# Summing the adaptive layer's weights on VectorE, 512 columns and one k-tile at a time, in place of GpSimd

## The chip, the cores and the metric

The kernel runs on one core of a Trainium2 chip, in one launch. The metric is device time in microseconds; the value of a kernel is the median of its runs. All times of single instructions below come from one execution that the hardware profiler took. The core's engines have one instruction queue each and wait for each other by semaphores: TensorE (PE) for matmuls, VectorE (DVE), ScalarE (ACT), GpSimd (POOL) and SyncE (SP, which here only issues DMAs).

## The reference

Two transformer blocks on 256 tokens of width 1024, all in float32. The first has two layers, each a feed-forward part, a mixer and another feed-forward part; the second is one layer of the same make, but every sublayer of it is modulated by a vector that comes from `c`. What the change touches is how that vector is made:

```python
mod = (jax.nn.silu(c) @ w_ada[l] + b_ada[l]).reshape(b, N_SUB, 3, D_MODEL)   # c: (1, 1024), w_ada[l]: (1024, 9216)
def sublayer(h, i, fn, resid_w):
    shift, scale, gate = mod[:, i, 0, None, :], mod[:, i, 1, None, :], mod[:, i, 2, None, :]
    u = rms_norm(h, norm_pre[l, i]) * (1.0 + scale) + shift
    return h + resid_w * gate * rms_norm(fn(u), norm_post[l, i])
h = sublayer(h, 0, ffn1, 0.5); h = sublayer(h, 1, token_mixer, 1.0); h = sublayer(h, 2, ffn2, 0.5)
```

The weights `w_ada` are 9216 columns of 1024 rows, 37.7 MB, used for one row of input.

## The kernel before

**Stages.** The program is a row of stages: six feed-forward stages of 11 chunks of 256 hidden columns, and the projections of the three mixers. A feed-forward stage is named here by the number of the norm ahead of it: norm 0, 2, 3, 5, 6 and 8. Norm 0, 2, 3 and 5 belong to the first block, norm 6 and 8 to the second.

**A chunk.** Each chunk takes three slots of weights of 128x2048 elements: slots 0 and 1 hold the up and gate weights, slot 2 the down weights. SP loads a slot into `raw`; ACT rounds it to `w_hi` (L1351, `split_hi`); DVE takes the rest, `w_lo` = `raw` - `w_hi` (L1875, `split_lo`); PE multiplies with three matmuls per product (L598 to L600, `three`). In one chunk PE runs `up` on slot 0 (24 matmuls), `up` on slot 1 (24) and `down` of the chunk before on slot 2 (24). DVE also multiplies the activated gate with the up half (L2038, `product`), transposes it by blocks (L2023, `blocks`), and, after four DMAs from ACT's queue and ACT's rounding (L1477), takes the rest of the turned hidden values, `hT_lo` (L2028, `turned_lo`). `middle(c)` writes DVE's order in one chunk: `w_lo` of slot 2, `hT_lo`, `w_lo` of slot 0, the two products, the transpose, `w_lo` of slot 1.

**The adaptive layer.** GpSimd works through 72 units of 128 columns. A unit is one DMA (L561, all eight k-tiles of the 128 columns, 512 KB) and four passes: multiply all 1024 elements of a partition by `c_silu` (L567), and add halves until 128 are left (L570, L572, L576). The loads alternate between two buffers, and unit n+2 is loaded when unit n is summed. Three units make 384 columns of `ada_acc`. DVE then folds them, in `fold(j)`: it waits for GpSimd's sum (`ada_summed`), transposes by blocks of 32 (L2047), and adds (L2050). There are 24 folds, six in each of the stages norm 2, 3, 5 and 6, after chunks 2, 3, 5, 6 and 8 (`FOLD_AT`) and after the last product. PE adds up what is left with four small matmuls (`ada_select`), at the start of the stages norm 5 and 6 and of the token mixer; the folds of a third must be done by then.

**When GpSimd works.** The first half of the units begins when the first mixer's output is turned for its projection and has 18 units before it waits for the stage norm 3 to begin (`actT_ready`), then 18 more; the second half does the same at the second mixer's output and at the stage norm 6.

**Queues.** Each engine takes its instructions in the written order. So a DVE fold that waits holds up every `w_lo` behind it, and `w_lo` is what PE waits for.

Of the kernel before, what the change touches and what calls it, by code (L numbers as in the profile page):

```python
# [167 lines left out]
def build(nc, a, out):  # L168
# [4 lines left out]
    with ctx:  # L173
# [173 lines left out]
        ada_scaled, ada_by4, ada_by2, ada_summed = (sem(n) for n in ("ada_scaled", "ada_by4", "ada_by2", "ada_summed"))  # L347
# [178 lines left out]
        def _(pool):  # L526
# [35 lines left out]

            def ada_unit(n):
                j, r = n // ADA_PER, ada_raw[:, n % 2, :, :]
                at = (n % ADA_PER) * ADA_U
                pool.wait_ge(ada_loaded[n % 2], 16 * (n // 2 + 1))
                nc.gpsimd.tensor_tensor(r, r, c_silu[:, :].unsqueeze(2).to_broadcast([P, KD, ADA_U]), ALU.mult)\  # L567
                    .then_inc(ada_scaled, 1)
                pool.wait_ge(ada_scaled, n + 1)
# [2070 lines left out]
```

## Time and profile before

| what | value |
|---|---|
| median of 3 runs | 1611.08 us (1610.66 to 1611.93) |
| span of the profiled execution, first to last instruction | 1609.3 us |
| what lies outside of the span, by the median of the runs | 1.8 us |
| PE busy | 98% |
| DVE busy | 72% |
| ACT busy | 51% |
| GpSimd busy | 38% |

The profiled execution's own time is not listed apart from the runs'; its span is 1.8 us under their median, and that distance is taken as what lies around a span. Busy shares are means over all stages. PE's instructions overlap in the records (each matmul is listed with about 390 ns and a new one begins every 226 ns or so), so PE counts as busy when it streams without a gap.

### The profile page before, as it was taken

What the parts mean: (1) busy time and instruction counts of PE and PEld (TensorE: products, weight loads), DVE (VectorE), ACT (ScalarE), POOL (GpSimd) and SP (SyncE); (2) the same over time, 40 slices, a digit from 0 to 9 for tenths busy, and PEclk for the clock granted to TensorE, in tenths of its full rate; (3) what the DMA queues carried; (4) which work ended last, traced back from release to release, by engine and by line L of the source; (5) the groups of instructions that cost most, each with busy time, mean ns of one, the idle gap of its engine ahead of it and who ended that gap; (6) DMA issues with size and microseconds to landing.
All of it is one profiled execution on the core that took longest, in us unless ns stands there. A gap on an engine that the chain in (4) does not pass through costs nothing.

```text
span 1609.3 us, 20974 instructions
## 1 busy us (share of the span) xinstructions
PE 1580.6 (98%) x7549; PEld 1303.2 (81%) x7549; DVE 1157.7 (72%) x1123; ACT 821.7 (51%) x984; POOL 615.5 (38%) x387
## 2 busy tenths in 40 slices
PE   7999999999999999999999999999999999999998
PEld 6888888888888788887887888888887888878887
DVE  5665668778877787876778787688798467775554
ACT  6465563354444544455665444554437566564443
POOL 2000100077993599930009898079992000000000
PEclk9999999999999999999999999999999999999999
DMA  8766663358887688865346889668884454447662
GB/s 268 232 208 214 215 209 105 105 174 274 268 276 222 207 277 262 271 198 191 124 139 220 282 257 282 217 192 272 259 278 162 156 174 146 170 144 222 205 219 86
DMA packets 242396, 337.25 MB, mean 210 GB/s; under 512 B 14185, under 2 KB 180290, under 8 KB 242336
## 3 DMA queue, kind: packets, MB, share of 16 engines
q1 hardware_dynamic: 196288, 281.05, 53.2%
q0 software_dynamic: 11280, 39.56, 7.9%
q10 hardware_dynamic: 34768, 15.83, 4.0%
q8 instruction: 37, 0.61, 0.2%
q14 instruction: 23, 0.19, 0.0%
HBM read 319.62 MB, written 1.05 MB: 199 GB/s over the span
## 4 chain that ended last, share of the span: by engine, by line
PE 79%; DVE 8%; POOL 6%; ACT 3%; issue 2%; DMA 1%; ACTq 1%; SPq 0%; DVEq 0%; POOLq 0%
PE ps L598 23%; PE ps L600 23%; PE ps L599 23%; DVE w_lo L1875 4%; PE ps L649 3%; POOL arena L570 2%; POOL arena L567 2%; PE ps L657 1%; PE ps L898 1%; ACT w_hi L1351 1%; PE ps L606 1%; POOL arena L572 1%; POOL arena L576 1%; DMA arena<-arena 1%; DVE arena L1907 1%
## 5 line engine op out<-in xcount | busy, mean ns | idle before, releaser
L1875 DVE TENSOR_TENSOR w_lo<-raw,w_hi 128x2048 fp32r<-128x2048 f32 x265 | 682.1, 2584 | 210.3 <-ACT w_hi L1351 209.8
L1351 ACT CAST w_hi<-raw 128x2048 fp32r<-128x2048 f32 x265 | 503.9, 1912 | 308.1 <-PE ps L600 255.7
L598 PE MATMUL ps<-w_hi,actT_hi 128*128 128x512 f32 x1456 | 572.0, 393 | 3.5 <-DVE w_lo L1875 2.5
L600 PE MATMUL ps<-w_hi,actT_lo 128*128 128x512 f32 x1456 | 567.0, 389 | 0.0
L599 PE MATMUL ps<-w_lo,actT_hi 128*128 128x512 f32 x1456 | 566.8, 389 | 0.0
L598 PEld LDWEIGHTS ps<-w_hi,actT_hi 128*128 128x128 f32 x1456 | 273.4, 188 | 63.4 <-issue 3.3
L600 PEld LDWEIGHTS ps<-w_hi,actT_lo 128*128 128x128 f32 x1456 | 273.3, 188 | 57.4
L599 PEld LDWEIGHTS ps<-w_lo,actT_hi 128*128 128x128 f32 x1456 | 273.5, 188 | 55.3
L570 POOL TENSOR_TENSOR arena<-arena 128x512 f32<-128x512 f32 x72 | 190.3, 2643 | 5.7
L567 POOL TENSOR_TENSOR arena<-arena,c_silu 128x1024 f32<-128x1024 f32 x72 | 153.6, 2133 | 100.6 <-DVE actT_lo L1910 49.9
L598 PE MATMUL ps<-w_hi,hT_hi 128*128 128x512 f32 x480 | 187.9, 391 | 1.6 <-DVE hT_lo L2028 1.6
L599 PE MATMUL ps<-w_lo,hT_hi 128*128 128x512 f32 x480 | 186.9, 389 | 0.0
L600 PE MATMUL ps<-w_hi,hT_lo 128*128 128x512 f32 x480 | 186.9, 389 | 0.0
L561 POOL DMA_DIRECT2D arena<-w_ada_dram x72 | 66.0, 917 | 295.7 <-PE ps L606 272.6
L2038 DVE TENSOR_TENSOR hidden<-gate,ps 128x256 f32<-128x256 f32 x132 | 76.7, 596 | 60.4 <-ACT gate L1486 53.9
L572 POOL TENSOR_TENSOR arena<-arena 128x256 f32<-128x256 f32 x72 | 109.5, 1521 | 5.6
L598 PEld LDWEIGHTS ps<-w_hi,hT_hi 128*128 128x128 f32 x480 | 90.1, 188 | 21.9 <-DVE hT_lo L2028 3.4
L600 PEld LDWEIGHTS ps<-w_hi,hT_lo 128*128 128x128 f32 x480 | 90.1, 188 | 18.9
L599 PEld LDWEIGHTS ps<-w_lo,hT_hi 128*128 128x128 f32 x480 | 90.1, 188 | 18.5
L1486 ACT ACTIVATE gate<-ps 128x256 f32<-128x256 f32 x66 | 25.3, 384 | 137.1 <-PE ps L600 116.7
L576 POOL TENSOR_TENSOR arena<-arena 128x128 f32<-128x128 f32 x72 | 80.4, 1117 | 17.4 <-DVE ada_fold L2050 12.0
L2028 DVE TENSOR_TENSOR hT_lo<-arena,hT_hi 128x512 fp32r<-128x512 f32 x60 | 72.8, 1213 | 4.2 <-ACT hT_hi L1477 4.1
(278 smaller groups left out, 1287.4 us busy)
## 6 DMA issues: line engine op xcount, KB each, us to landing
raw<-ffn_w_in_dram SPq DMA_DIRECT2D x174, 512.0 KB, 5.0
raw<-ffn_w_out_dram SPq DMA_DIRECT2D x88, 512.0 KB, 4.6
arena<-w_ada_dram POOLq DMA_DIRECT2D x72, 512.0 KB, 6.4
raw<-ffn_w_gate_dram SPq DMA_DIRECT2D x44, 512.0 KB, 4.0
raw<-ffn_w_up_dram SPq DMA_DIRECT2D x44, 512.0 KB, 5.1
raw<-ffn_w_down_dram SPq DMA_DIRECT2D x44, 512.0 KB, 4.4
raw<-w_in_dram SPq DMA_DIRECT2D x40, 512.0 KB, 4.8
raw<-hg_w_in_dram SPq DMA_DIRECT2D x32, 512.0 KB, 5.0
```

What stands on the lines that cost most here:

```text
L561: nc.gpsimd.dma_start(ada_raw[:, n % 2, :, :], w_ada[:, :, n * ADA_U:(n + 1) * ADA_U]).then_inc(ada_loaded[n % 2], 16)
L567: nc.gpsimd.tensor_tensor(r, r, c_silu[:, :].unsqueeze(2).to_broadcast([P, KD, ADA_U]), ALU.mult)\
L570: nc.gpsimd.tensor_tensor(r[:, 0:4, :], r[:, 0:4, :], r[:, 4:8, :], ALU.add).then_inc(ada_by4, 1)
L572: nc.gpsimd.tensor_tensor(r[:, 0:2, :], r[:, 0:2, :], r[:, 2:4, :], ALU.add).then_inc(ada_by2, 1)
L576: nc.gpsimd.tensor_tensor(ada_acc[j % 2][:, at:at + ADA_U], r[:, 0, :], r[:, 1, :], ALU.add).then_inc(ada_summed, 1)
L598: nc.tensor.matmul(to, hi, whi, start=start, stop=False, skip_group_check=True)
L599: nc.tensor.matmul(to, hi, wlo, start=False, stop=False, skip_group_check=True)
L600: return nc.tensor.matmul(to, lo, whi, start=False, stop=stop, skip_group_check=True)
L1351: nc.scalar.copy(w_hi[:, s, :], raw[:, s, :]).then_inc(hi_ready[s], 1)
L1875: nc.vector.tensor_tensor(w_lo[:, s, :], raw[:, s, :], w_hi[:, s, :].bitcast(F32), ALU.subtract)\
L2028: nc.vector.tensor_tensor(hT_lo.rearrange("p f t -> p (f t)").rearrange("p (n a j) -> p n a j", n=4, a=4), hT_columns, hT_hi.bitcast(F32). ...
L2038: nc.vector.tensor_tensor(to, g, u, ALU.mult).then_inc(hidden_ready, 1)
```

## The change

The unit is cut the other way. A unit is now two k-tiles of 512 columns (again 512 KB, again 72 units), and four units give 512 finished columns. For each k-tile DVE runs one pass over 512 columns: for the first of eight `ada_acc = part * c_silu[k]`, for the other seven `ada_acc = part * c_silu[k] + ada_acc`. That is 144 passes, 36 in each of the stages norm 2, 3, 5 and 6: one unit (two passes) in `middle(c)` between `hT_lo` and `w_lo` of slot 0, and one after `middle(c)`, for the chunks 1 to 9. Each pass waits for the one before it by `ada_added`, and the first of a unit for its load. A fold takes 512 columns; there are 18 of them, each right after the unit that ends its 512 columns, and none after the last product. GpSimd keeps only the 72 DMA issues, each after the unit two before it is added.

```diff
-ADA_U = 128
-ADA_PER = 3
-ADA_FOLD = ADA_PER * ADA_U
-FOLD_AT = (2, 3, 5, 6, 8)
+ADA_FOLD = 512
+ADA_KS = 2
+ADA_PER = KD // ADA_KS
+FOLDS = 3 * ADA_W // ADA_FOLD
+ADA_UNITS = FOLDS * ADA_PER
+ADA_IN = {2: 0, 3: 18, 5: 36, 6: 54}
...
-                pool.wait_ge(ada_loaded[n % 2], 16 * (n // 2 + 1))
-                nc.gpsimd.tensor_tensor(r, r, c_silu[:, :].unsqueeze(2).to_broadcast([P, KD, ADA_U]), ALU.mult)\
-                nc.gpsimd.tensor_tensor(r[:, 0:4, :], r[:, 0:4, :], r[:, 4:8, :], ALU.add).then_inc(ada_by4, 1)
-                nc.gpsimd.tensor_tensor(r[:, 0:2, :], r[:, 0:2, :], r[:, 2:4, :], ALU.add).then_inc(ada_by2, 1)
-                nc.gpsimd.tensor_tensor(ada_acc[j % 2][:, at:at + ADA_U], r[:, 0, :], r[:, 1, :], ALU.add).then_inc(ada_summed, 1)
...
+            for n in range(ADA_UNITS):
+                if n == ADA_UNITS // 2:
                     pool.wait_ge(turned, 4 * (by_name["fox_out"].turned + 1))
+                elif n % (ADA_UNITS // 2) >= 2:
+                    pool.wait_ge(ada_added, ADA_KS * (n - 1))
+                j, ks = n // ADA_PER, n % ADA_PER * ADA_KS
+                nc.gpsimd.dma_start(ada_raw[:, n % 2, :, :], w_ada[:, ks:ks + ADA_KS, j * ADA_FOLD:(j + 1) * ADA_FOLD])\
+                    .then_inc(ada_loaded[n % 2], 16)
...
+                def ada_add(n):
+                    acc_j = ada_acc[n // ADA_PER % 2]
+                    dve.wait_ge(ada_loaded[n % 2], 16 * (n // 2 + 1))
+                    for kk in range(ADA_KS):
+                        k, part = n % ADA_PER * ADA_KS + kk, ada_raw[:, n % 2, kk, :]
+                        if k == 0:
+                            total = nc.vector.tensor_scalar(acc_j, part, c_silu[:, k:k + 1], None, ALU.mult)
+                        else:
+                            dve.wait_ge(ada_added, ADA_KS * n + kk)
+                            total = nc.vector.scalar_tensor_tensor(acc_j, part, c_silu[:, k:k + 1], acc_j, ALU.mult, ALU.add)
+                        total.then_inc(ada_added, 1)
...
-                        middle(c)
+                        unit = ADA_IN[st.norm] + 2 * (c - 1)
+                        middle(c, lambda: ada_add(unit))
+                        ada_add(unit + 1)
...
-                        if c in FOLD_AT:
-                            fold(FOLD_IN[st.norm] + FOLD_AT.index(c))
+                        if unit % ADA_PER:
+                            fold(unit // ADA_PER)
```

VectorE's queue in chunk 2 of the stage norm 2, from `hT_lo` to the first fold and the `w_lo` of slot 2 behind it, before (`hi_ready0`, `1` and `2` name the slots; `arena<-arena` of 128x384 is the fold's transpose):

```order
L2028 TENSOR_TENSOR hT_lo<-arena,hT_hi 128x512 [waits hT_hi_ready]
L1875 TENSOR_TENSOR w_lo<-raw,w_hi 128x2048 [waits hi_ready0]
L2038 TENSOR_TENSOR hidden<-gate,ps 128x8x32 [waits gate_ready] x2
L2023 STREAM_TRANSPOSE arena<-hidden 128x512 [waits hT_loaded,hidden_ready]
L1875 TENSOR_TENSOR w_lo<-raw,w_hi 128x2048 [waits hi_ready1]
L2047 STREAM_TRANSPOSE arena<-arena 128x384 [waits ada_summed]
L2050 TENSOR_REDUCE ada_fold<-arena 128x12 [waits ada_block]
L1875 TENSOR_TENSOR w_lo<-raw,w_hi 128x2048 [waits hi_ready2,ada_folded]
```

Here nothing of the adaptive layer but the fold stands in the queue. And now, the same piece of the same chunk:

```order
L2003 TENSOR_TENSOR hT_lo<-arena,hT_hi 128x512 [waits hT_hi_ready]
L2031 SCALAR_TENSOR_TENSOR arena<-arena,c_silu 128x512 [waits ada_added,ada_loaded0]
L2031 SCALAR_TENSOR_TENSOR arena<-arena,c_silu 128x512 [waits ada_added]
L1850 TENSOR_TENSOR w_lo<-raw,w_hi 128x2048 [waits hi_ready0]
L2013 TENSOR_TENSOR hidden<-gate,ps 128x8x32 [waits gate_ready] x2
L1998 STREAM_TRANSPOSE arena<-hidden 128x512 [waits hT_loaded,hidden_ready]
L1850 TENSOR_TENSOR w_lo<-raw,w_hi 128x2048 [waits hi_ready1]
L2031 SCALAR_TENSOR_TENSOR arena<-arena,c_silu 128x512 [waits ada_added,ada_loaded1]
L2031 SCALAR_TENSOR_TENSOR arena<-arena,c_silu 128x512 [waits ada_added]
L2037 STREAM_TRANSPOSE arena<-arena 128x512 [waits ada_added]
L2040 TENSOR_REDUCE ada_fold<-arena 128x16 [waits ada_block]
L1850 TENSOR_TENSOR w_lo<-raw,w_hi 128x2048 [waits hi_ready2,ada_folded]
```

Two passes now stand ahead of slot 0's `w_lo` and two behind slot 1's, and the fold waits for VectorE's own passes and no longer for GpSimd's.

GpSimd's queue at the first unit, before, two loads ahead and then passes and loads in turn:

```order
L561 DMA arena<-w_ada_dram 128x8x128 [waits c_ready,turned]
L561 DMA arena<-w_ada_dram 128x8x128
L567 TENSOR_TENSOR arena<-arena,c_silu 128x1024 [waits ada_loaded0]
L570 TENSOR_TENSOR arena<-arena 128x512 [waits ada_scaled]
L572 TENSOR_TENSOR arena<-arena 128x256 [waits ada_by4]
L576 TENSOR_TENSOR arena<-arena 128x128 [waits ada_by2]
L561 DMA arena<-w_ada_dram 128x8x128 [waits ada_summed]
```

And now, both halves and the bias that follows them:

```order
L564 DMA arena<-w_ada_dram 128x2x512 [waits turned]
L564 DMA arena<-w_ada_dram 128x2x512
L564 DMA arena<-w_ada_dram 128x2x512 [waits ada_added] x34
L564 DMA arena<-w_ada_dram 128x2x512 [waits turned]
L564 DMA arena<-w_ada_dram 128x2x512
L564 DMA arena<-w_ada_dram 128x2x512 [waits ada_added] x34
L566 DMA arena<-da_bias_dram 128x1536
```

All four passes are gone from this queue, and what a load waits for is VectorE.

## Rows read from the trace of the kernel before

**Rows 1.** The page: span, then engines with busy us, share and instructions.

```profile
span 1609.3 us, 20974 instructions
PE 1580.6 (98%) x7549; PEld 1303.2 (81%) x7549; DVE 1157.7 (72%) x1123; ACT 821.7 (51%) x984; POOL 615.5 (38%) x387
```

**Rows 2.** Windows, inside norm 6 and norm 8: busy us (instructions) by engine, PEclk, DMA.

```profile
1053.00:1217.00 164.00, 161.29 (x716) 132.32 (x715) 134.72 (x87) 73.20 (x65) 153.13 (x89) 1.00 0.82 260
1440.00:1590.00 150.00, 150.00 (x663) 124.17 (x663) 88.94 (x66) 65.37 (x58) 0.00 (x0) 1.00 0.65 205
```

**Rows 3.** Waits of PE from 326 to 1222 us: total us, times, longest.

```profile
PE ps L606 <- DVE arena L1916: 2.0, 5, 0.4
PE ps L598 <- DVE w_lo L1875: 1.7, 1, 1.7
PE ps L598 <- DVE hT_lo L2028: 1.6, 3, 0.7
PE ps L706 <- DVE hidden L2038: 1.4, 1, 1.4
```

**Rows 4.** Timeline of VectorE at those waits: start, us, instruction [idle before].

```profile
348.21 1.77 DVE L1916 TENSOR_SCALAR arena<-x,small 128x1024 f32<-128x1024 f32 x1
...
364.29 3.43 DVE L1875 TENSOR_TENSOR w_lo<-raw,w_hi 128x2048 fp32r<-128x2048 f32 x1 [1.85 <-ACT w_hi L1351]
...
543.40 8.10 DVE L1875 TENSOR_TENSOR w_lo<-raw,w_hi 128x2048 fp32r<-128x2048 f32 x2 [0.43 <-ACT w_hi L1351]
...
1061.73 3.40 DVE L1875 TENSOR_TENSOR w_lo<-raw,w_hi 128x2048 fp32r<-128x2048 f32 x1
...
1159.27 0.58 DVE L2047 STREAM_TRANSPOSE arena<-arena 128x384 f32<-128x384 f32 x1 [6.21 <-POOL arena L576]
...
1209.97 2.11 DVE L2028 TENSOR_TENSOR hT_lo<-arena,hT_hi 128x512 fp32r<-128x512 f32 x1 [1.55 <-ACT hT_hi L1477]
1212.01 3.39 DVE L1875 TENSOR_TENSOR w_lo<-raw,w_hi 128x2048 fp32r<-128x2048 f32 x1
```

**Rows 5.** Groups of the page: count, then busy us, mean ns, idle before.

```profile
L1875 DVE TENSOR_TENSOR w_lo<-raw,w_hi 128x2048 fp32r<-128x2048 f32 x265 | 682.1, 2584 | 210.3 <-ACT w_hi L1351 209.8
L1351 ACT CAST w_hi<-raw 128x2048 fp32r<-128x2048 f32 x265 | 503.9, 1912 | 308.1 <-PE ps L600 255.7
L570 POOL TENSOR_TENSOR arena<-arena 128x512 f32<-128x512 f32 x72 | 190.3, 2643 | 5.7
L561 POOL DMA_DIRECT2D arena<-w_ada_dram x72 | 66.0, 917 | 295.7 <-PE ps L606 272.6
```

**Rows 6.** The same groups for VectorE, 1440 to 1590 us, GpSimd idle.

```profile
L1875 DVE TENSOR_TENSOR w_lo<-raw,w_hi 128x2048 fp32r<-128x2048 f32 x29 | 66.5, 2292 | 50.5 <-ACT w_hi L1351 50.5
```

**Rows 7.** Timeline of VectorE, one chunk of norm 8, GpSimd idle.

```profile
1452.89 2.29 DVE L1875 TENSOR_TENSOR w_lo<-raw,w_hi 128x2048 fp32r<-128x2048 f32 x1 [2.88 <-ACT w_hi L1351]
1455.10 0.69 DVE L2028 TENSOR_TENSOR hT_lo<-arena,hT_hi 128x512 fp32r<-128x512 f32 x1
1458.38 2.29 DVE L1875 TENSOR_TENSOR w_lo<-raw,w_hi 128x2048 fp32r<-128x2048 f32 x1 [2.60 <-ACT w_hi L1351]
1460.59 0.60 DVE L2038 TENSOR_TENSOR hidden<-gate,ps 128x256 f32<-128x256 f32 x1
1462.24 0.63 DVE L2038 TENSOR_TENSOR hidden<-gate,ps 128x256 f32<-128x256 f32 x1 [1.05 <-ACT gate L1486]
1463.00 0.71 DVE L2023 STREAM_TRANSPOSE arena<-hidden 128x512 f32<-128x512 f32 x1
1464.04 2.29 DVE L1875 TENSOR_TENSOR w_lo<-raw,w_hi 128x2048 fp32r<-128x2048 f32 x1 [0.32 <-ACT w_hi L1351]
```

**Rows 8.** VectorE groups whose shapes are those of the added work: mean ns.

```profile
L2448 DVE TENSOR_REDUCE small<-arena 128x2 f32<-128x512 f32 x4 | 2.7, 676 | 0.0
L1966 DVE SCALAR_TENSOR_TENSOR x<-arena,small,x 128x512 f32<-128x512 f32 x4 | 2.8, 748 | 0.1
```

**Rows 9.** Loads of `w_ada` (L561), from issue to landing.

```profile
DMA to landing us min/median/max: 4.5/6.4/8.6
```

More of the change, by code:

```diff
@@ L50 @@
 ADA_W = 3 * D
-ADA_U = 128
-ADA_N = ADA_W // ADA_U
-ADA_PER = 3
-ADA_FOLD = ADA_PER * ADA_U
-FOLDS = 3 * ADA_N // ADA_PER
-FOLD_IN = {2: 0, 3: 6, 5: 12, 6: 18}
-FOLD_AT = (2, 3, 5, 6, 8)
+ADA_N = ADA_W // P
+ADA_FOLD = 512
[4 more added lines that the diff above has]
+ADA_IN = {2: 0, 3: 18, 5: 36, 6: 54}
 FOX_IN = 4 * D + FOX_H
@@ L248, in build @@
         rows_a, rows_b = region(8704, P), region(8832, P)
-        ada_raw = region(5120, 2, KD, ADA_U)
+        ada_raw = region(5120, 2, ADA_KS, ADA_FOLD)
         ada_acc = [region(8192 + ADA_FOLD * i, ADA_FOLD) for i in range(2)]
-        ada_turned = region(8192 + 2 * ADA_FOLD, ADA_FOLD)
+        ada_turned = region(10624, ADA_FOLD)
         ada_sel = lb[:, 0:4, :].rearrange("p a b -> p (a b)")
@@ L346, in build @@
         ada_loaded = [sem("ada_loaded0"), sem("ada_loaded1")]
-        ada_scaled, ada_by4, ada_by2, ada_summed = (sem(n) for n in ("ada_scaled", "ada_by4", "ada_by2", "ada_summed"))
+        ada_added = sem("ada_added")
         ada_block, ada_folded, sel_ready = sem("ada_block"), sem("ada_folded"), sem("sel_ready")
@@ L579, in _ @@
-            half = 3 * ADA_N // 2
-            for first in (0, half):
-                if first:
-                    pool.wait_ge(turned, 4 * (by_name["fox_out"].turned + 1))
-                ada_load(first)
-                ada_load(first + 1)
-                for n in range(first, first + half):
-                    if n == first + half // 2:
-                        pool.wait_ge(actT_ready, 4 * ((8 if first else 4) + 1))
-                    ada_unit(n)
-                    if n + 2 < first + half:
-                        ada_load(n + 2)
+            for n in range(ADA_UNITS):
+                if n == ADA_UNITS // 2:
+                    pool.wait_ge(turned, 4 * (by_name["fox_out"].turned + 1))
+                elif n % (ADA_UNITS // 2) >= 2:
[3 more added lines that the diff above has]
+                    .then_inc(ada_loaded[n % 2], 16)
@@ L2053, in fold, with middle @@
                     dve.wait_ge(ada_folded, j + 1)
-                def middle(c):
+                def middle(c, between=None):
                     split_lo(2, filled[2] + c - 1)
                     turned_lo(c - 1)
+                    if between is not None:
+                        between()
                     split_lo(0, filled[0] + c)
@@ L2083, in ffn @@
                 product(NF - 1, False)
-                if st.norm in FOLD_IN:
-                    fold(FOLD_IN[st.norm] + len(FOLD_AT))
                 last_lo(st, 0)
```

19 lines of the change are left out of this document (4 added, 15 removed).

## The prediction, made before the change was run

> **What bounds the kernel now.** I read the page's head first. PE is busy 98% of a span of 1609.3 us, DVE 72%, GpSimd 38% [rows 1]. Then the windows: between 1440 and 1590 us, where no adaptive work runs, PE streams 663 matmuls in 150 us without a gap, 0.226 us each; inside norm 6, beside GpSimd, it lacks 2.7 of 164 us [rows 2]. So PE's stream sets the time, and nothing that is done on another engine can return more than PE's gaps in the stretches it touches. The view of waits gives these gaps. From 326 us to 1222 us, the stretch in which GpSimd has adaptive work, PE waited 2.0 + 1.7 + 1.6 + 1.4 = 6.7 us for VectorE's instructions named there [rows 3]. The timeline of VectorE at these waits tells why: each stands behind a DVE instruction that took longer than its like. Where GpSimd is idle a `w_lo` takes 2.29 us [rows 6] and an `hT_lo` 0.69 us [rows 7]. Over the whole program a `w_lo` takes 2.58 us on average [rows 5]; at the waits two took 8.10 us together, others 3.4 us, an `hT_lo` 2.11 us, and one fold stood still for 6.21 us on GpSimd's sum [rows 4].
>
> **What the change removes.** GpSimd's four passes per unit. Its busy time of 615.5 us [rows 1] falls by all but the 66.0 us of issues [rows 5] and a few early instructions. On GpSimd itself this is worth nothing. On DVE it is worth the slowing: 682.1 us of `w_lo` [rows 5] less 265 x 2.292 us [rows 6] is 74.7 us.
>
> What of it lies on PE's path I take wait by wait.
> 1. The turns (L606) that wait for L1916: 2.0 us in five, the longest 0.4 us [rows 3]. Two of the five stand where GpSimd computes, at 349 and 861 us; the first has a scaling of 1024 columns of 1.77 us ahead of it [rows 4], which at the rate of an undisturbed `w_lo` (2048 columns in 2.29 us) would take 1.15 us at most; that is 0.6 us of slowing against a wait of 0.4 us. These two go: 0.8 us. The other three stand at the ends of norm 2, 3 and 5, with GpSimd idle, and stay.
> 2. L598 waits 1.7 us for `w_lo` at 546 us. The first `w_lo` of the 8.10 us pair began at 543.40 and would end at 545.7 us at 2.29 us. PE wants it at 546.3 us. It goes: 1.7 us, with 0.6 us to spare.
> 3. L598 waits 1.6 us for `hT_lo`, three times: behind the `w_lo` of 3.43 us (364 us), behind the one of 3.40 us (1061 us), and after the fold that stood 6.21 us (1159 us). At 2.29 and 0.69 us the first two come 1.1 us + 0.5 us earlier than they did, against waits of at most 0.7 us; the third fold waits no longer for GpSimd. They go: 1.6 us.
> 4. The last product of norm 6 is 1.4 us late (L706), behind an `hT_lo` of 2.11 and a `w_lo` of 3.39 us: 1.4 + 1.1 = 2.5 us of slowing. It goes: 1.4 us.
>
> The sum is 0.8 + 1.7 + 1.6 + 1.4 = 5.5 us.
>
> **What it adds on VectorE.** The three-operand pass over 128x512 floats in SBUF stands in the trace, at 748 ns [rows 8]. A pass that waits for the one before it needs a little more; I take 0.79 us for every pass, 1.6 us for a unit and 144 x 0.79 = 114 us in all. This is the near bound. From above I know only that a pass of 512 columns next to GpSimd's work could be slowed as `w_lo` was, by 3.39 / 2.29 = 1.5 times, 1.2 us; GpSimd computes nothing now, so I take the near bound. The folds: 18 x (0.71 us for a transpose of 512 [rows 7] + 0.68 us for the reduce [rows 8]) = 25 us, in place of 24 smaller ones, about the same. DVE's busy time thus rises by 114 - 75 = 39 us at most, less what `hT_lo` gets back; it stays near 73% of the span.
>
> Is there room for it in a chunk? A chunk of PE is 72 matmuls, 72 x 0.226 = 16.3 us. DVE's undisturbed work in it is 3 x 2.29 + 0.69 + 0.60 + 0.63 + 0.71 = 9.5 us, and the four gaps in its timeline are 2.88 + 2.60 + 1.05 + 0.32 = 6.9 us [rows 7]. Four passes take 3.2 us, and a fold 1.4 us in every second chunk: 4.6 us at most. They also stand where the gaps are. The first unit comes ahead of slot 0's `w_lo`, which had 2.60 us of idle before it: 1.6 us fits. The second unit and the fold come ahead of slot 2's `w_lo`, which had 2.88 us: 3.0 us makes this one 0.1 us late. In chunk 4 of norm 5 the gate's diagonal comes too, some 2 us, and makes it 2 us late.
>
> What is late next if they don't fit? Each slot is used for 24 matmuls, 5.4 us, and then has 16.3 - 5.4 = 10.9 us in which ACT rounds (1.91 us [rows 5]) and DVE subtracts (2.29 us). So 6.6 us are left before PE misses it, and a delay of 2 or 3 us in DVE costs PE nothing. That is the cover of all 144 passes: I cost them at 0 us.
>
> The tightest place is chunk 1 of each of the four stages. There DVE is behind from the stage's turn, and product 1, which PE needs before it may overwrite the up bank in chunk 2, comes after the first unit. In norm 3 I put PE's need at 557.4 us (the stream 1.7 us earlier) and the product's end at 556.0 us: `w_lo` of slot 2 after its rounding to 550.3, `hT_lo` to 551.0, the unit to 552.6, `w_lo` of slot 0 to 554.9, two products to 556.0. 1.4 us are left there and about as many or more in the three others. No new wait, but this is the first place for one.
>
> **The loads.** GpSimd now issues load n+2 when DVE has added unit n, and DVE needs it one chunk later, 16.3 us less the unit's own 1.6. An issue takes 0.92 us [rows 5] and the landing 4.5 to 8.6 us [rows 9]: at most 9.5 us. 5 us are left, so DVE never stands at a load. Were it to, everything behind it in the queue would stand too: slot 0's or slot 2's `w_lo`, and PE after them. The bytes are the same, spread over nearly the same time. The bias load behind the last unit only moves earlier, into the end of norm 6, where its region is free.
>
> **The skill against the rows.** `w_lo` and `hT_lo` are slow only beside GpSimd's passes, a `w_lo` 2.58 us over all against 2.29 us alone [rows 5, 6]. The Trainium skill, page "SBUF — State Buffer", section "Who interferes with whom", has the rule: a VectorE instruction with two inputs in SBUF contends with a GpSimd instruction that reads SBUF, and whichever starts first holds the shared ports to its end; the trace agrees. The same section speaks against the change: an fp32 `tensor_scalar` can take both ports and keep GpSimd from writing a load's descriptors. By that rule the 18 first passes could hold back an issue; the sum stays the same, since a load has 5 us to spare.
>
> **The rivals.**
> - *Part of the waits stay.* DVE is not idle at the four places of the sum now; the units take their part of what the slowing gives back. The `hT_lo` waits and the last product's (1.6 + 1.4 us) stand late in DVE's order, and at the last product ACT's `hT_hi` was itself late by a DMA (1.55 us of idle [rows 4]). If these 3.0 us stay, the gain is 2.5 us: 1611.1 - 2.5 = 1608.6. For it: the last fold now comes ahead of slot 2's `w_lo`. Against: the slowing that goes is larger than each wait. Chance 0.2.
> - *GpSimd's issues disturb DVE as much as its passes.* Then the change does only part of what it says. 74.7 us of slowing over some 549 us of passes is 0.14 us per us; 66 us of issues would cost 9 us of DVE time, 0.25 us per chunk. It hides in the gaps: the forecast's time again, and counted with it.
> - *More comes back.* Every DVE-bound wait in the stretch goes, also the three turns of 0.4 us, and transfers of 2 KB runs in place of 512 B ones relieve raw loads that are now late at the stages' starts. At most 2.5 us more: 1603.1. Chance 0.08.
> - *Slower: the passes fill the chunk.* The place is DVE's queue between slot 0's and slot 2's `w_lo`. It decides when DVE's chunk exceeds PE's: (16.3 - 9.5 - 0.7) / 4 = 1.52 us per pass. At 1.75 us per pass the chunk is 17.2 us, 0.9 us more, and over 36 chunks 32 us, less 5.5: 1637.6. It needs passes twice as long as the row's 748 ns. The wait from pass to pass through a semaphore is what could do it, or a load that lands later than 14 us. Chance 0.05.
>
> **The numbers.** The runs' median is 1611.1 us, 1.8 us above the span of 1609.3; gaps of PE's stream carry over one to one. Forecast: 1611.1 - 5.5 = 1605.6 us, chance 0.67 (the second rival included). For 8 times in 10 the range takes the forecast with its neighbours on both sides: 1603.0 from the third rival, and 1609.4 from the first with 0.8 us for a new wait in one or two first chunks. A measurement of this kernel can tell 0.2%, 3.2 us, from no change: below 1607.9 is faster, above 1614.3 slower. Faster gets the forecast without its upper edge, 0.63, and the third rival, 0.08: 0.71. Slower gets the fourth, 0.05, and 0.02 for new waits in all four stages' starts. Same has the rest, 0.22.
>
> **What will show it.** After the change `w_lo` should take 2.29 us in all stages and DVE's passes 0.75 to 0.8 us; PE's waits for `w_lo` near 546 us, for `hT_lo` three times and for the last product of norm 6 should be gone from the view of waits; slot 0's and slot 2's `w_lo` should have lost most of their idle time and PE's windows inside norm 2 to 6 should read full. GpSimd's busy time should be under 80 us. What would make the forecast wrong: passes above 1.5 us, DVE standing at a load, PE waiting for product 1 at the head of chunk 2, or a `w_lo` that stays slow with GpSimd idle.

## The result

The changed kernel takes 1602.91 us (median of 5 runs, 1601.55 to 1604.88) against 1611.08 us before; the ratio is 0.9946, 95% interval 0.9935 to 0.9956, a gain of 7.1 to 10.5 us. Forecast were 1605.6 us and a range from 1603.0 to 1609.4. The direction was right, the gain was larger than the forecast 5.5 us, and the time lies just under the range.

The page of the changed kernel, head and the groups that answer to [rows 1] and [rows 5] (count, then busy us, mean ns, idle before):

```profile
span 1603.1 us, 20837 instructions
PE 1580.2 (99%) x7549; PEld 1305.7 (81%) x7549; DVE 1139.3 (71%) x1255; ACT 818.6 (51%) x984; POOL 66.7 (4%) x99
...
L1850 DVE TENSOR_TENSOR w_lo<-raw,w_hi 128x2048 fp32r<-128x2048 f32 x265 | 604.0, 2289 | 199.4 <-ACT w_hi L1326 198.4
...
L2031 DVE SCALAR_TENSOR_TENSOR arena<-arena,c_silu 128x512 f32<-128x512 f32 x126 | 94.4, 749 | 2.5
L564 POOL DMA_DIRECT2D arena<-w_ada_dram x72 | 51.2, 711 | 938.0 <-DVE arena L2031 634.1
```

The changed kernel's lines stand 25 lower here (L1875 is L1850, L2028 is L2003). VectorE has 132 instructions more and 18.4 us less busy time than before: `w_lo` takes 2.29 us everywhere, 78 us less in sum, `hT_lo` 32 us less in sum (72.8 before, 41.1 now), and the added passes take 94.4 us and 18 x 0.48 us. GpSimd is busy for 66.7 us. The view of waits for PE from 326 to 1222 us, which answers to [rows 3], has none of its four rows left:

```profile
PE ps L573 <- ACT arena L1607: 0.7, 1, 0.7
PE ps L987 <- DVE hT_lo L2275: 0.5, 1, 0.5
```

Both stand in the second mixer and stood there before. The windows inside norm 2, 3 and 6 show PE busy without a gap beside a VectorE that is busy for 79 to 80% of the time (columns as in [rows 2]):

```profile
370.00:510.00 140.00, 140.00 (x619) 115.99 (x618) 110.95 (x106) 60.23 (x53) 12.79 (x18) 1.00 0.88 288
545.00:695.00 150.00, 150.00 (x664) 124.20 (x663) 120.47 (x113) 66.44 (x57) 11.37 (x16) 1.00 0.85 277
1050.00:1212.00 162.00, 162.00 (x723) 133.76 (x722) 128.38 (x125) 73.94 (x65) 11.92 (x17) 1.00 0.83 274
```

One chunk of norm 6 in VectorE's timeline shows where the passes went, beside [rows 7]:

```profile
1089.40 1.53 DVE L2031 SCALAR_TENSOR_TENSOR arena<-arena,c_silu 128x512 f32<-128x512 f32 x2
1092.08 2.29 DVE L1850 TENSOR_TENSOR w_lo<-raw,w_hi 128x2048 fp32r<-128x2048 f32 x1 [1.15 <-ACT w_hi L1326]
1094.29 0.60 DVE L2013 TENSOR_TENSOR hidden<-gate,ps 128x256 f32<-128x256 f32 x1
1095.94 0.62 DVE L2013 TENSOR_TENSOR hidden<-gate,ps 128x256 f32<-128x256 f32 x1 [1.04 <-ACT gate L1461]
1096.59 0.71 DVE L1998 STREAM_TRANSPOSE arena<-hidden 128x512 f32<-128x512 f32 x1
1097.74 2.29 DVE L1850 TENSOR_TENSOR w_lo<-raw,w_hi 128x2048 fp32r<-128x2048 f32 x1 [0.44 <-ACT w_hi L1326]
1099.95 1.53 DVE L2031 SCALAR_TENSOR_TENSOR arena<-arena,c_silu 128x512 f32<-128x512 f32 x2
1101.52 0.71 DVE L2037 STREAM_TRANSPOSE arena<-arena 128x512 f32<-128x512 f32 x1
1102.26 0.69 DVE L2040 TENSOR_REDUCE ada_fold<-arena 128x16 f32<-128x512 f32 x1
1102.98 2.29 DVE L1850 TENSOR_TENSOR w_lo<-raw,w_hi 128x2048 fp32r<-128x2048 f32 x1
```

The idle of 2.60 us before slot 0's `w_lo` has become 1.15 us, that of 2.88 us before slot 2's is gone. A pair of passes takes 1.53 us, a little less than the 1.6 us of the prediction.

### The profile page after: what moved, and what is told of

Its sections match the earlier page's. It is cut to its first block, busy times and chain, and to the rows that moved or that the text cites. A ratio compares the mean times of both kernels' runs of the same rounds, so it can differ in the third digit from the quotient of the medians.

```text
span 1603.1 us, 20837 instructions
## 1 busy us (share of the span) xinstructions
PE 1580.2 (99%) x7549; PEld 1305.7 (81%) x7549; DVE 1139.3 (71%) x1255; ACT 818.6 (51%) x984; POOL 66.7 (4%) x99
## 4 chain that ended last, share of the span: by engine, by line
PE 94%; DVE 3%; ACT 2%; DMA 1%; issue 0%; SPq 0%; DVEq 0%; ACTq 0%
PE ps L573 27%; PE ps L575 27%; PE ps L574 27%; PE ps L624 4%; PE ps L632 2%; PE ps L873 1%; PE ps L581 1%; DVE w_lo L1850 1%; ACT w_hi L1326 1%; DMA raw<-ffn_w_in_dram 1%; PE ps L1143 0%; PE ps L1005 0%; PE ps L1031 0%; PE ps L806 0%; DVE arena L1882 0%
## 5 line engine op out<-in xcount | busy, mean ns | idle before, releaser
L1850 DVE TENSOR_TENSOR w_lo<-raw,w_hi 128x2048 fp32r<-128x2048 f32 x265 | 604.0, 2289 | 199.4 <-ACT w_hi L1326 198.4
L573 PE MATMUL ps<-w_hi,actT_hi 128*128 128x512 f32 x1456 | 571.9, 393 | 1.8 <-DVE w_lo L1850 0.8
L574 PE MATMUL ps<-w_lo,actT_hi 128*128 128x512 f32 x1456 | 566.7, 389 | 0.0
L1461 ACT ACTIVATE gate<-ps 128x256 f32<-128x256 f32 x66 | 25.3, 384 | 143.0 <-PE ps L575 122.5
L2031 DVE SCALAR_TENSOR_TENSOR arena<-arena,c_silu 128x512 f32<-128x512 f32 x126 | 94.4, 749 | 2.5
L564 POOL DMA_DIRECT2D arena<-w_ada_dram x72 | 51.2, 711 | 938.0 <-DVE arena L2031 634.1
L624 PE MATMUL ps<-w_hi,actT_hi 128*128 128x512 f32 x144 | 59.3, 412 | 3.6 <-ACT actT_hi L1345 1.9
L624 PE MATMUL ps<-w_lo,actT_hi 128*128 128x512 f32 x144 | 58.1, 404 | 0.0
L1457 ACT ACTIVATE gate<-ps 128x256 f32<-128x256 f32 x66 | 25.3, 383 | 54.1 <-PE ps L575 54.0
L1998 DVE STREAM_TRANSPOSE arena<-hidden 128x512 f32<-128x512 f32 x60 | 42.7, 711 | 3.8
```

Of the source, the lines that this page charges most:

```text
L564: nc.gpsimd.dma_start(ada_raw[:, n % 2, :, :], w_ada[:, ks:ks + ADA_KS, j * ADA_FOLD:(j + 1) * ADA_FOLD])\
L573: nc.tensor.matmul(to, hi, whi, start=start, stop=False, skip_group_check=True)
L574: nc.tensor.matmul(to, hi, wlo, start=False, stop=False, skip_group_check=True)
L624: nc.tensor.matmul(to, actT_hi[:, k, tok], half[:, s, w], start=k == 0 and half is w_hi, stop=False, skip_group_check=True)
L1457: nc.scalar.activation(gate[:, 0, :], ps[:, UP_BANK, 0:FC], ACT.Silu).then_inc(gate_ready, 1)
L1850: nc.vector.tensor_tensor(w_lo[:, s, :], raw[:, s, :], w_hi[:, s, :].bitcast(F32), ALU.subtract)\
```

## Where the 9.5 us are: both traces side by side

PE issues the same 7549 matmuls in the same order in both kernels. So the start of each can be set against the start of the same one before, and every place where the distance changes is a place where time was lost or won. Up to 17.6 us after the start the changed kernel's trace falls 3.2 us behind (more on it with the first experiment); from there to the end it wins 9.5 us. The large steps are these, with the idle time that the trace of before gives at the same place:

| us in the trace of before | PE waits before for | idle listed, us | won there, us | in the forecast |
|---|---|---|---|---|
| 350 | scaling, L1916 | 0.36 | 0.57 | yes |
| 369 | `hT_lo` | 0.37 | 0.66 | yes |
| 548 | `w_lo` | 1.68 | 2.02 | yes |
| 861 | scaling, L1916 | 0.40 | 0.62 | yes |
| 1066 | `hT_lo` | 0.70 | 1.04 | yes |
| 1165 | `hT_lo` | 0.54 | 0.88 | yes |
| 1216 | last product, L2038 | 1.45 | 1.64 | yes |
| 527, 711, 1038 | scaling, L1916 | 0.41, 0.40, 0.41 | 0.63, 0.61, 0.63 | no |

What is won is the distance between the two streams some 2 us before a wait less that 3 us behind it, when both step evenly again. The seven forecast places give 7.4 us where their idle time sums to 5.5 us. The three others give 1.9 us. Some 0.2 us are spread over small steps. All of this is one execution against one; the third experiment shows that two of the seven waits, at 1165 and 1216 us, are not in every execution of the kernel before.

PE's timeline before, at 546 us, tells why a wait costs more than its idle time (start, us, instruction, and in brackets the idle time):

```profile
546.19 0.39 PE L600 MATMUL ps<-w_hi,actT_lo 128*128 128x512 f32 x1
548.26 0.50 PE L598 MATMUL ps<-w_hi,actT_hi 128*128 128x512 f32 x1 [1.68 <-DVE w_lo L1875]
548.60 0.40 PE L599 MATMUL ps<-w_lo,actT_hi 128*128 128x512 f32 x1
548.84 0.40 PE L600 MATMUL ps<-w_hi,actT_lo 128*128 128x512 f32 x1
549.08 0.40 PE L598 MATMUL ps<-w_hi,actT_hi 128*128 128x512 f32 x1
```

In a running stream a matmul starts every 0.227 us. Here the step over the wait is 2.07 us, 1.84 us too long, the next is 0.34 us, 0.11 us too long, and those after it are a hundredth long each for a while. The records give a matmul 0.39 us, so 0.16 us of the wait are counted as busy. By the table a wait costs 0.2 to 0.35 us beyond its listed idle time.

## Experiments

### The changed kernel again

> The changed kernel again, as the base for the three runs beside it. In the profiles the change is 6.2 us shorter, by the medians 8.2 us. Setting the two traces' PE instructions side by side, one by one, gives another split: 3.2 us are lost by 17.6 us after the start, in PE's first matmuls, and 9.6 us are won after it. Theory A (the first 18 us differ from execution to execution and have nothing to do with the change): the medians will again be 8 to 9.6 us apart, and this profile's first matmuls will take another time than the last one's. Theory B (the change costs 3 us at the start): the same 3 us will stand in this profile's first 18 us.

Measured: 1603.31 us (1601.67 to 1604.02) against 1611.51; ratio 0.9943 (0.9929 to 0.9957). The profiled execution has a span of 1601.3 us, and its PE stream is that of the first one from 20 us on, shifted by 1.7 us. PE's timeline shows what the shift is, in the first trace of the changed kernel and then in this one:

```profile
16.96 0.63 PE L624 MATMUL ps<-w_lo,actT_hi 128*128 128x512 f32 x1
17.39 0.63 PE L624 MATMUL ps<-w_hi,actT_hi 128*128 128x512 f32 x1
...
19.52 0.63 PE L624 MATMUL ps<-w_lo,actT_hi 128*128 128x512 f32 x1
```

```profile
15.51 0.63 PE L624 MATMUL ps<-w_lo,actT_hi 128*128 128x512 f32 x1
15.93 0.63 PE L624 MATMUL ps<-w_hi,actT_hi 128*128 128x512 f32 x1
...
18.07 0.63 PE L624 MATMUL ps<-w_lo,actT_hi 128*128 128x512 f32 x1
```

The first matmuls step by 0.43 us, nearly twice 0.227 (the view of windows gives a granted clock of 1.00 there in both traces, so only the steps show it), and how long this lasts and how long PE waits in between differs between executions of one kernel. Theory A holds. The second stage's first matmul, which was at 195.9 us before and at 199.1 us after the change, stood at 197.4, 196.5, 197.7 and 195.9 us in the traces of this run and the next three, of which the third (197.7) is a variant of the kernel before and the others are of the changed one. So 3.2 us of distance between two profiles say nothing of the change, and the 9.5 us that are won behind it lie inside the interval of the runs, 7.1 to 10.5 us.

### The fold put back behind the last product

```diff
-                        if unit % ADA_PER:
+                        if unit % ADA_PER and c < 8:
                             fold(unit // ADA_PER)
...
                 product(NF - 1, False)
+                if st.norm in ADA_IN:
+                    fold((ADA_IN[st.norm] + 18) // ADA_PER - 1)
```

> The changed kernel with the last fold of each of the four stages (norm 2, 3, 5, 6) moved behind the last product, where the kernel before had one. Theory A: what the prediction missed is that fold. It stood in VectorE's queue ahead of the residual and the scaling for which PE's turn (L606, three waits of 0.4 us at the ends of norm 2, 3 and 5) waited. Then these three waits come back, at 0.5 to 0.6 us each with the restart of PE's stream, and the run is 1.5 to 2 us longer than the changed kernel, 1604.5 to 1605 us. Theory B: GpSimd's passes slowed VectorE there too; then the three waits stay away and the time is the changed kernel's.

Measured: 1604.54 us (1604.23 to 1606.08), 1.2 us over the changed kernel beside it. PE's stream lost 0.9 us at each of the ends of norm 2, 3 and 5, 2.65 us in all, and kept its distance everywhere else behind the start, within 0.1 us. That is more than the 0.6 us at each of these places before; the fold is longer now, 1.40 us (0.71 + 0.69) against 1.12. The medians are only 1.2 us apart, but the ranges of the runs taken side by side do not touch. At the end of norm 6, where a fold came back too, nothing moved: PE waits there 1.08 us for the scaling before the change and 1.06 us after it. The row that is new among PE's waits from 326 to 1222 us:

```profile
PE ps L581 <- DVE arena L1891: 1.5, 3, 0.5
```

The three waits are back, with GpSimd idle: theory A. VectorE's timelines at the end of norm 2 show how. Before the change:

```profile
516.89 0.57 DVE L2047 STREAM_TRANSPOSE arena<-arena 128x384 f32<-128x384 f32 x1
517.50 0.55 DVE L2050 TENSOR_REDUCE ada_fold<-arena 128x12 f32<-128x384 f32 x1
518.09 0.42 DVE L2094 TENSOR_TENSOR hT_last_lo<-ps,hT_last_hi 128x256 fp32r<-128x256 f32 x1
518.43 4.48 DVE L1875 TENSOR_TENSOR w_lo<-raw,w_hi 128x2048 fp32r<-128x2048 f32 x2
522.83 1.28 DVE L1944 SCALAR_TENSOR_TENSOR x<-ps,x 128x512 f32<-128x512 f32 x2
```

and in the changed kernel:

```profile
518.95 0.42 DVE L2086 TENSOR_TENSOR hT_last_lo<-ps,hT_last_hi 128x256 fp32r<-128x256 f32 x1
519.28 4.48 DVE L1850 TENSOR_TENSOR w_lo<-raw,w_hi 128x2048 fp32r<-128x2048 f32 x2
524.19 1.29 DVE L1919 SCALAR_TENSOR_TENSOR x<-ps,x 128x512 f32<-128x512 f32 x2 [0.42 <-PE ps L575]
```

Behind the last product VectorE has no idle time: `hT_last_lo`, two `w_lo` and the residual follow at once. Whatever stands ahead of them moves the residual, and with it the norm and the turn for which PE waits. Without the fold the residual waits for PE, as it should.

### The kernel before, its last fold earlier in two stages

```diff
+                        if c == NF - 2 and st.norm in (2, 5):
+                            fold(FOLD_IN[st.norm] + len(FOLD_AT))
...
-                if st.norm in FOLD_IN:
+                if st.norm in (3, 6):
                     fold(FOLD_IN[st.norm] + len(FOLD_AT))
```

> The kernel before with one change: in norm 2 and norm 5 the last fold stands after chunk 9 and not behind the last product. GpSimd is idle there, its sums are done. Theory A (the fold at the stage's end is on PE's path): the waits of the turn at 526 and 1037 us go, that at 711 us stays, and the run is 1.0 to 1.2 us faster than the kernel before. Theory B: nothing moves.

Measured: 1610.47 us (12 runs, 1608.4 to 1613.88) against 1611.51; ratio 0.9993 (0.9984 to 1.0003). The times alone don't tell 1 us from nothing. The traces do: the turns at 527 and 1038 us each came 0.63 us earlier, that at 711 us did not move, and PE's row of waits for L1916 fell from 2.0 us in five to this:

```profile
PE ps L606 <- DVE arena L1916: 1.2, 3, 0.5
```

So the fold's place costs what theory A says. In norm 6 this execution also lost 2.5 us less than the profile of before, at the waits of 1165 and 1216 us, where nothing was edited. The fold that stood 6.21 us before stands 2.55 us here, and the `w_lo` behind it takes 4.06 us in place of 2.29:

```profile
1157.49 0.58 DVE L2047 STREAM_TRANSPOSE arena<-arena 128x384 f32<-128x384 f32 x1 [2.55 <-POOL arena L576]
...
1158.69 4.06 DVE L1875 TENSOR_TENSOR w_lo<-raw,w_hi 128x2048 fp32r<-128x2048 f32 x1
```

How GpSimd's passes fall between VectorE's is different here, and with it whether PE waits. So 2.5 of the 9.5 us in the table belong to the one execution that was profiled; how often these two waits are there is not known. The medians' 8.2 us lie between 9.5 and the 7.0 us without them.

### The passes over 8 columns in place of 512

```diff
-                        k, part = n % ADA_PER * ADA_KS + kk, ada_raw[:, n % 2, kk, :]
+                        k, part = n % ADA_PER * ADA_KS + kk, ada_raw[:, n % 2, kk, 0:8]
...
-                    acc_j = ada_acc[n // ADA_PER % 2]
+                    acc_j = ada_acc[n // ADA_PER % 2][:, 0:8]
```

> The changed kernel with the 144 passes over 8 of the 512 columns of a k-tile in place of all (504 columns of each sum are left out; loads, waits, folds and their places are kept). Theory A (the passes are hidden in VectorE's gaps): the time is the changed kernel's within 0.5 us, 1602.9. Theory B (the passes cost something that the lost contention outweighs): it is faster by that much, 1 to 4 us. VectorE's busy time falls by some 75 us either way.

Measured: 1603.44 us (1601.55 to 1603.74), the changed kernel's 1603.31 within 0.2. From the second stage's first matmul to the end of the span are 1403.9 us, in the changed kernel 1404.0. A pass over 8 columns still takes 0.224 us, so the run takes away 70 of the 103 us of passes and leaves 32; these 70 us cost PE nothing: theory A. That the rest costs nothing follows from the view of waits, in which no wait for VectorE is left that was not in the second mixer before.

### The kernel before, with GpSimd's passes made into memsets

```diff
-                nc.gpsimd.tensor_tensor(r, r, c_silu[:, :].unsqueeze(2).to_broadcast([P, KD, ADA_U]), ALU.mult)\
-                    .then_inc(ada_scaled, 1)
+                step(nc.gpsimd.memset(r, 0.0))
+                step(nc.gpsimd.memset(r, 0.0))
+                nc.gpsimd.memset(r, 0.0).then_inc(ada_scaled, 1)
...
-                nc.gpsimd.tensor_tensor(r[:, 0:4, :], r[:, 0:4, :], r[:, 4:8, :], ALU.add).then_inc(ada_by4, 1)
+                step(nc.gpsimd.memset(r, 0.0))
+                nc.gpsimd.memset(r, 0.0).then_inc(ada_by4, 1)
...
+                step(nc.gpsimd.memset(r, 0.0))
+                nc.gpsimd.memset(r[:, 0:4, :], 0.0).then_inc(ada_by2, 1)
...
+                nc.gpsimd.memset(ada_acc[j % 2][:, at:at + ADA_U], 0.0).then_inc(ada_summed, 1)
```

> The kernel before, with GpSimd's four passes of each unit replaced by seven and a half memsets of up to 1024 columns and one of 128 (the adaptive layer's sums are left out; loads, semaphores, folds and their places are kept, and a unit takes GpSimd about as long). By the run with memsets GpSimd's writes alone leave VectorE alone. So this takes away the slowing and keeps the folds' waits on GpSimd and the fold behind the last product. Theory A (the slowing made the waits at 350, 368, 548, 861, 1066 and 1215 us, and a wait costs PE 0.1 to 0.3 us more than its listed idle time because the stream restarts): these go, 0.5 + 0.7 + 2.0 + 0.6 + 1.0 + 1.6 = 6.4 us, the three turns of 0.6 us stay, the wait at 1165 us may stay: 1605.1 us. Theory B (half of it came from VectorE's standing at the folds): 1608.

Measured: 1604.83 us (1604.28 to 1606.33) against 1611.53; ratio 0.9964, interval 0.995 to 0.9977, which spans 3.7 to 8.1 us. `w_lo` takes 2.29 us, GpSimd is still busy for 547 us, and of the four rows of PE's waits from 326 to 1222 us one is left:

```profile
PE ps L609 <- DVE arena L1919: 1.8, 5, 0.4
```

Five waits of at most 0.4 us for the scaling are left, also the two at 350 and 861 us, which theory A had as gone. Their scaling has one SBUF input and still met memsets: it took 1.59 and 1.78 us, against 0.75 us in the changed kernel. The wait at 1165 us is gone too. Side by side with the trace of before, PE's stream wins 6.7 us, 6.2 of them at the waits of 369, 548, 1066, 1165 and 1216 us.

The run does not keep what it was meant to keep, the folds' waits. The edit has six and a half memsets of 1024 columns per unit, not the seven and a half of the expectation, and a unit takes GpSimd 6.5 us in place of 7.4. So no fold waits for GpSimd in it. Before, six did, and this row is gone from VectorE's waits:

```profile
DVE arena L2047 <- POOL arena L576: 10.3, 6, 6.2
```

These six are at 644, 674, 1105, 1159, 1189 and 1217 us. None stands ahead of the waits at 369, 548 and 1066 us in their stages, so there the slowing alone is left as the cause, 3.7 us with the restarts. Between the waits at 1165 and 1216 us there is only one of 0.35 us, against 2.5 us of slowing just ahead of the last product. At 1165 us the slowing and the fold's stand of 6.21 us go together in this run, and which of them PE's 0.9 us are due to isn't shown. They are not independent either: GpSimd's own passes vary in length beside VectorE's (one pass of L570 takes between 1.28 and 3.31 us for the same work), and long ones make its sums late. So theory A is shown for four of its six waits. Theory B can't be judged by the time alone, since the folds' stands went too; the places of these stands speak against it for the same four.

### GpSimd's passes put back, on data nobody needs

```diff
                 nc.gpsimd.dma_start(ada_raw[:, n % 2, :, :], w_ada[:, ks:ks + ADA_KS, j * ADA_FOLD:(j + 1) * ADA_FOLD])\
                     .then_inc(ada_loaded[n % 2], 16)
...
+                if n % (ADA_UNITS // 2) >= 2:
+                    step(nc.gpsimd.tensor_tensor(idle, idle, c_silu[:, :].unsqueeze(2).to_broadcast([P, KD, 128]), ALU.mult))
+                    step(nc.gpsimd.tensor_tensor(idle[:, 0:4, :], idle[:, 0:4, :], idle[:, 4:8, :], ALU.add))
+                    step(nc.gpsimd.tensor_tensor(idle[:, 0:2, :], idle[:, 0:2, :], idle[:, 2:4, :], ALU.add))
+                    nc.gpsimd.tensor_tensor(idle[:, 0, :], idle[:, 0, :], idle[:, 1, :], ALU.add).then_inc(idle_done, 1)
...
+                if st.norm in (3, 6):
+                    dve.wait_ge(idle_done, 34 if st.norm == 3 else 68)
```

> The changed kernel, and after each load from the third of a half on GpSimd runs the four passes of the kernel before (1024, 512, 256 and 128 columns) on a scratch region that nobody reads; VectorE waits for them only behind the last product of norm 3 and 6. So nothing waits for GpSimd, and only its company is put back. Theory A (GpSimd's passes slow VectorE's instructions with two SBUF inputs, and that made PE's waits): w_lo averages 2.5 to 2.6 us again over the whole program, the added passes rise from 0.75 to about 1 us, a chunk of VectorE holds 9.5 + 3.2 + 0.7 + some 2.5 = 15.9 of 16.3 us, and some of PE's waits at the starts of the four stages come back: 1605 to 1609 us. Theory B (what cost time was that VectorE stood at GpSimd's sums, not the slowing): w_lo is slow, the time stays at 1603.

Measured: 1645.3 us (1642.94 to 1647.27) against 1612.36; ratio 1.0202 (1.0185 to 1.0219). It is theory A's mechanism, and its size was forecast far too small. VectorE's groups:

```profile
L1859 DVE TENSOR_TENSOR w_lo<-raw,w_hi 128x2048 fp32r<-128x2048 f32 x265 | 639.2, 2422 | 129.0 <-ACT w_hi L1335 128.0
L2040 DVE SCALAR_TENSOR_TENSOR arena<-arena,c_silu 128x512 f32<-128x512 f32 x126 | 163.8, 1300 | 2.6
L2012 DVE TENSOR_TENSOR hT_lo<-arena,hT_hi 128x512 fp32r<-128x512 f32 x60 | 85.0, 1416 | 5.8 <-ACT hT_hi L1461 5.7
```

The passes took 1.30 us in place of 0.75. Against the changed kernel VectorE is busy 149.5 us longer (1288.8 us), 4.2 us per chunk of the 36. With 9.5 + 3.1 + 0.7 that is 17.5 us where PE needs 16.3: 1.2 us too long, 43 us over the chunks. From the second stage's start on PE's stream was 43.8 us longer. VectorE stood 2.6 us before these passes in all, so the loads, which now stand behind GpSimd's passes in its queue, were not what held it. The added work fits only because GpSimd's went.

### GpSimd writing, not reading

The edit is the one above with five memsets of 1024 columns in place of the four passes.

```diff
+                    for width in (1024, 1024, 1024, 1024):
+                        step(nc.gpsimd.memset(idle_flat[:, 0:width], 0.0))
+                    nc.gpsimd.memset(idle_flat[:, 0:1024], 0.0).then_inc(idle_done, 1)
...
```

> As the run with GpSimd's passes, but GpSimd writes zeros (five memsets of 1024 columns per load) where it ran passes: it is busy and writes SBUF, and reads none. Theory A (the slowing comes from reads through a shared port, as the Trainium skill, page "SBUF — State Buffer", section "Who interferes with whom", states): w_lo stays at 2.29 us and the time at the changed kernel's 1603. Theory B (any GpSimd work slows VectorE): w_lo above 2.4 us.

Measured: 1602.46 us (1601.76 to 1603.45), as the changed kernel. VectorE's groups:

```profile
L1856 DVE TENSOR_TENSOR w_lo<-raw,w_hi 128x2048 fp32r<-128x2048 f32 x265 | 603.8, 2288 | 191.3 <-ACT w_hi L1332 190.3
L2037 DVE SCALAR_TENSOR_TENSOR arena<-arena,c_silu 128x512 f32<-128x512 f32 x126 | 94.3, 749 | 2.5
L2034 DVE TENSOR_SCALAR arena<-arena,c_silu 128x512 f32<-128x512 f32 x18 | 19.1, 1063 | 0.0
```

328.7 us of memsets leave `w_lo` and the three-operand passes alone. By that rule of the Trainium skill ("SBUF — State Buffer", "Who interferes with whom") a GpSimd instruction that only writes doesn't meet a VectorE instruction with two SBUF inputs; the runs agree. The last row is its other half. A `tensor_scalar` with one SBUF input takes 1063 ns beside memsets, 481 ns in the changed kernel:

```profile
L2028 DVE TENSOR_SCALAR arena<-arena,c_silu 128x512 f32<-128x512 f32 x18 | 8.7, 481 | 0.0
```

The same section says that a `tensor_scalar` can run in a mode that takes the port pair shared with GpSimd, and then contends with it; the 1063 ns agree.

### Where the room ends

```diff
...
+                        for _ in range(1):
+                            step(nc.vector.scalar_tensor_tensor(ada_twice, part, c_silu[:, k:k + 1], acc_j, ALU.mult, ALU.add))
                         if k == 0:
                             total = nc.vector.tensor_scalar(acc_j, part, c_silu[:, k:k + 1], None, ALU.mult)
```

> The changed kernel with one more three-operand pass of 512 columns ahead of each of the 144 (written to a scratch region, waited for). This tests where the room in VectorE's chunk ends. By the prediction's sum a chunk is then 9.5 + 8 x 0.79 + 0.7 = 16.5 us on VectorE against 16.3 on PE: just over, at most 0.2 us x 36 chunks = 8 us, and up to 2 us in each stage's first chunk, 1603 to 1618 us. Rival: the chunk's waits (gate, rounding) don't overlap with the passes and the room ends earlier; then it is 1 to 2 us per chunk, 1640 to 1675.

Measured: 1607.87 us (10 runs, 1604.96 to 1612.34), 4.6 to 5 us over the changed kernel and inside what was expected. The profiled execution is the slowest of the ten, 1612.34 us, and its stream is 9.2 us longer than the changed kernel's, so the sizes below are more than the median has. In it norm 2 and 3 lose nothing. The loss begins in chunk 4 of norm 5, where the gate's diagonal comes on top, 2 us in four steps, and then stands at the last products of norm 5 and 6. PE's timeline at the first of them:

```profile
1028.93 0.66 PE L682 MATMUL ps<-consts_sb,hidden 128*128 128x128 f32 x2 [3.04 <-DVE hidden L2014]
...
1029.81 0.63 PE L575 MATMUL ps<-w_lo,hT_hi 128*128 128x512 f32 x1
1030.24 0.63 PE L576 MATMUL ps<-w_hi,hT_lo 128*128 128x512 f32 x1
...
1032.24 0.40 PE L575 MATMUL ps<-w_lo,hT_hi 128*128 128x512 f32 x1
```

and the window over it (columns as in [rows 2]):

```profile
1026.00:1034.00 8.00, 5.07 (x18) 4.17 (x19) 6.92 (x6) 6.13 (x8) 0.00 (x0) 0.79 0.42 135
```

After 3.04 us of idle time the matmuls step by 0.43 us until 1032 us, and the granted clock of the window is 0.79: part of it lies at the lower of the two levels, 1.2 GHz. The wait costs 3.3 us and the slow stream behind it another 1.5 us. The wait at the end of norm 6, 2.01 us idle, is followed by steps of 0.23 us almost at once, and the granted clock stays at 1.00.

The same with two more passes ahead of each (`range(2)`):

> The same with two more passes ahead of each. The chunk on VectorE is 9.5 + 12 x 0.79 + 0.7 = 19.7 us, 3.4 us over PE's, in 36 chunks 122 us: about 1725 us. If VectorE's queue is the bound then, PE's waits for w_lo and hT_lo hold all of it. Rival: above 1750, if waits add to the queue.

Measured: 1706.34 us in one run. The stream is 103.0 us longer than the changed kernel's, 2.9 us per chunk in place of 3.4. The difference is the price of a pass: 0.75 us was measured, the forecast took 0.79, and 9.5 + 12 x 0.75 + 0.7 = 19.2 us is 2.9 over 16.3. PE's waits:

```profile
PE ps L574 <- DVE hidden L2014: 46.4, 34, 1.6
PE ps L574 <- DVE hT_lo L2004: 21.7, 17, 2.2
PE ps L682 <- DVE hidden L2014: 12.1, 4, 3.8
```

VectorE's queue is the bound here, and PE meets it first at the product and at `hT_lo`, not at `w_lo`, in which the forecast also placed it. Between one and two extra passes of 0.75 us per k-tile the cost turns from a few us to 100. So the end of the room lies between 1.5 and 2.25 us per k-tile, and the chunk's sum, which put it at 1.52, gives the cost of the second run right.

## Why the prediction was right, and where it was wrong

**What bounds the kernel** was right. PE's gaps are all that moved; between them both streams step by 0.227 us.

**What the change removes** was right in its cause and too small in its sum, in two terms.

The first is the size of a wait. The prediction took the idle time that the trace lists before a PE instruction as what PE loses, and summed 5.5 us. The same seven places gave 7.4 us. The failed step is "gaps of PE's stream carry over one to one": the listed gap begins when the record of the last matmul ends, 0.16 us after the next one would have begun, and the stream takes a few matmuls to be at its step again. The rows of before showed it, in the starts.

The second is a place left out. "The other three stand at the ends of norm 2, 3 and 5, with GpSimd idle, and stay" was wrong; they gave 1.9 us where it had nothing. The prediction asked only who was slowed there, not what else the change takes out of the queue. The description of the change says that there is no fold after the last product, and the prediction counts the folds only by their sum, 25 us against 27. That fold stood at the one stretch of a stage where VectorE has no idle time. Both fold experiments show it, one by taking it away from the kernel before (0.63 us at each of two), one by giving it back to the changed one (0.9 us at each of three). The third rival, "more comes back", named these three turns and got 0.08. That its 1603.1 is near the measured 1602.9 is in part luck: it counted the turns at 1.2 us and the rest to raw loads at the stages' starts, of which the streams side by side show next to nothing, and the size of the waits is not in it. The range's lower end was set at it, with nothing below for the size of a wait.

Within the first term the split among the causes holds for the most part: the run with memsets wins 6.7 us by medians with all folds in place. That this is near the 6.4 us expected of it is luck, since the waits at 350 and 861 us stayed (1.2 us) and the one at 1165 us went (0.9 us). Whether the one at 1165 us is the slowing's or, as the prediction has it, that of the fold that stood 6.21 us is open. At 350 and 861 us the scaling, one SBUF input, still met memsets: there GpSimd's writing is enough. And the waits at 1165 and 1216 us were missing in another execution of nearly the same kernel, so 2.0 of the 5.5 us were not a fixed price.

**What it adds** was right for PE: 144 passes at 0 us. A pass took 0.749 us (0.748 taken from the row, 0.79 with its wait; the wait costs 0.02 to 0.04 us), narrowing them to 8 columns won nothing, VectorE's busy time fell by 18.4 us where up to 39 more was forecast (the passes took 103 us, not 114, and the slowing gave back more than the 75 us of `w_lo`), and the idle times before slot 0's and slot 2's `w_lo` shrank as forecast. No product was late at the head of a chunk 2. The threshold of 1.52 us per pass lies between the runs with one and with two extra passes, nearer to the first.

**The loads** were right. VectorE never stood at one; an issue takes 0.71 us and a load lands after 4.1 to 7.8 us, median 5.2, against 0.92 and 6.4 us before ([rows 5], [rows 9]). No issue took longer than 0.73 us, so none was held back by a first pass in a way that its length shows.

**The rivals.** *Part of the waits stay*: no, none did. *GpSimd's issues disturb VectorE*: no, `w_lo` is at 2.29 us with 51.2 us of issues beside it. *Slower, the passes fill the chunk*: the mechanism is real, as the runs with more passes and with GpSimd's passes put back show, and its point was right; the kernel is at half of it.

## What to carry to other kernels

When one engine streams and sets the time, list its waits and price each by the starts of its instructions around it, not by the idle time beside it; the difference was a third here. Before work is moved onto a busy in-order engine, look for its idle time between the very instructions it will stand between, per period and with the shortest deadline behind it, and look too at what the change takes out of stretches with no idle time: a fold of 1.1 us there was worth 0.6 us at each of three stage ends. And passes on GpSimd that read SBUF are paid for on VectorE: 534 us of them cost it over 100 us, and the 103 us of passes that do the same work on VectorE itself added nothing to PE's time.

## What the runs showed of the hardware

- GpSimd passes that read SBUF slowed VectorE instructions with two SBUF inputs, from 2.29 to 4.9 us at most for one `w_lo`, and from 0.75 to 1.30 us on average for a three-operand pass; GpSimd memsets did not (749 ns). A `tensor_scalar` with one SBUF input did meet memsets, from 481 to 1063 ns. GpSimd's passes varied too: one of 512 columns (L570) took from 1.28 to 3.31 us in the kernel before.
- After 3.04 us without a matmul PE ran at nearly twice its step for 3 us, at a granted clock of 0.79 over that window of 8 us. After 2.01 us, in the same run, and after 1.7 us, the longest wait in mid-program before the change, it stayed at 1.00.
- The first matmuls of an execution step by 0.43 us, and the time until the stream is at 0.227 us differs by up to 3 us between executions: more than a third of the change measured here.
